# Two small gaps in on-chip memory: the arena moved by 64 bytes and the weight buffers by 96, in a 256-token transformer kernel

## The reference

```
# first block
p = rms_norm(x) @ w_in                 # 2048 -> 5632 and 8 gate columns
y = mixers(p) @ w_out                  # gated delta rule, RG-LRU, SGU, short conv; 2048 -> 2048
x = x + rms_norm(y)
y = (gelu(gate) * val) @ ffn_down      # gate, val = conv(rms_norm(x) @ ffn_up); 2048 -> 2*5632 -> 2048
x = x + rms_norm(y)
# second block
x = x + 0.5 * swiglu(rms_norm(x), ffn1_w_gate, ffn1_w_up, ffn1_w_down)
proj = rms_norm(x) @ w_in_2            # dilated and differential attention, two gates
y = sigmoid(g_dil) * (o_dil @ w_dil_branch) + sigmoid(g_diff) * (o_diff @ w_diff_branch)
x = x + y @ w_out_2
x = x + 0.5 * swiglu(rms_norm(x), ffn2_w_gate, ffn2_w_up, ffn2_w_down)
```

## Time and profile before

| | |
|---|---|
| time, median of three runs | 3381.89 us |
| profiled execution, first to last instruction | 3379.9 us |
| PE busy | 3364.0 us |
| DVE / ACT / POOL busy | 2240.8 / 1745.9 / 533.6 us |
| DMA | 616 MB, mean share of the 16 DMA engines about 57% |
| granted TensorE clock, mean | 0.999 |

### The profile page before, as it was taken

One profiled execution on the slowest core, in us unless ns is written; L12 is line 12 of the kernel. 1 busy time (PEld: TensorE's weight loads), 2 busy tenths in 40 slices (PEclk: granted clock), 3 DMA queues, 4 the chain that ended last, 5 costly groups with the idle time before them and its releaser, 6 DMA issues.

```text
span 3379.9 us, 59341 instructions
## 1 busy us (share of the span) xinstructions
PE 3364.0 (100%) x19746; PEld 2935.0 (87%) x19746; DVE 2240.8 (66%) x2874; ACT 1745.9 (52%) x2588; POOL 533.6 (16%) x502
## 2 busy tenths in 40 slices
PE   9999999999999999999999999999999999999999
PEld 8888888888888888888888888888888888888888
DVE  7878587777744565656555599766687655655544
ACT  5555665555544554454444555554565554444433
POOL 0214111111100011111100066511100111111000
PEclk9999999999999999999999999999999999999999
DMA  6534555555566555555566655545566555555665
GB/s 212 162 113 156 185 170 186 187 190 188 183 193 189 175 179 191 187 189 187 186 190 187 217 176 174 190 154 160 168 195 197 189 187 189 187 186 192 183 193 171
DMA packets 176036, 616.21 MB, mean 182 GB/s; under 512 B 20912, under 2 KB 21584, under 8 KB 175568
## 3 DMA queue, kind: packets, MB, share of 16 engines
q1 hardware_dynamic: 175520, 609.84, 56.6%
q10 hardware_dynamic: 432, 5.24, 0.4%
HBM read 610.81 MB, written 4.19 MB: 182 GB/s over the span
## 4 chain that ended last, share of the span: by engine, by line
PE 94%; DVE 3%; issue 1%; ACT 1%; SPq 1%; DMA 0%; POOL 0%; DVEq 0%; POOLq 0%; ACTq 0%
PE acc L461 60%; PE acc L464 30%; DVE weights_low L311 1%; PE ps_wide L390 1%; PE acc L476 1%; ACT weights_high L304 0%; PE ps_narrow L2550 0%; PE ps_wide L2526 0%; PE acc L479 0%; DVE halves_memory L566 0%; DMA weights_raw<-in_w_in 0%; DMA weights_raw<-in_w_diff_branch 0%; DVE halves_memory L3009 0%; PE ps_scale L2931 0%; PE ps_wide L2537 0%
## 5 line engine op out<-in xcount | busy, mean ns | idle before, releaser
L461 PE MATMUL acc<-moving_halves,weights_high 128*128 128x512 f32 x6304 | 1994.5, 398 | 1.7 <-DVE x_T L2819 1.7
L311 DVE TENSOR_TENSOR weights_low<-weights_raw,weights_high 128x1024 fp32r<-128x1024 f32 (+1 forms) x1172 | 1433.8, 1236 | 728.4 <-ACT weights_high L304 726.8
L304 ACT ACTIVATE weights_high<-weights_raw 128x1024 fp32r<-128x1024 f32 (+1 forms) x1172 | 1208.5, 1032 | 786.0 <-PE acc L464 756.1
L464 PEld LDWEIGHTS acc<-moving_halves,weights_low 128*128 128x128 f32 x6304 | 1184.9, 188 | 280.1
L464 PE MATMUL acc<-moving_halves,weights_low 128*128 128x256 f32 x6304 | 1239.7, 278 | 0.0
L461 PEld LDWEIGHTS acc<-moving_halves,weights_high 128*128 128x128 f32 x6304 | 962.9, 189 | 12.0 <-issue 9.8
L461 PE MATMUL acc<-gated_halves,weights_high 128*128 128x512 f32 x2024 | 635.6, 395 | 0.0
L560 ACT ACTIVATE cross_products<-acc 128x256 f32<-128x256 f32 x503 | 192.5, 383 | 678.6 <-PE acc L464 678.5
L464 PEld LDWEIGHTS acc<-gated_halves,weights_low 128*128 128x128 f32 x2024 | 380.2, 188 | 89.9
L583 POOL TENSOR_TENSOR stage_scratch<-unscaled,token_scale 128x256 f32<-128x256 f32 x260 | 215.6, 829 | 1293.6 <-DVE unscaled L566 811.8
L464 PE MATMUL acc<-gated_halves,weights_low 128*128 128x256 f32 x2024 | 397.6, 278 | 0.0
(11 more groups left out here) (384 smaller groups left out, 2011.1 us busy)
## 6 DMA issues: line engine op xcount, KB each, us to landing
weights_raw<-in_w_in SPq DMA_DIRECT2D x268, 512.0 KB, 3.9
weights_raw<-in_ffn_up SPq DMA_DIRECT2D x176, 512.0 KB, 4.4
weights_raw<-in_ffn_w_gate SPq DMA_DIRECT2D x176, 512.0 KB, 4.1
weights_raw<-in_ffn_w_up SPq DMA_DIRECT2D x176, 512.0 KB, 4.7
weights_raw<-in_ffn_w_down SPq DMA_DIRECT2D x160, 512.0 KB, 3.8
weights_raw<-in_ffn_down SPq DMA_DIRECT2D x80, 512.0 KB, 3.8
weights_raw<-in_w_out SPq DMA_DIRECT2D x64, 512.0 KB, 4.1
weights_raw<-in_ffn_w_down SPq DMA_DIRECT2D x32, 256.0 KB, 2.7
```

The lines of the kernel that those rows point to most:

```text
L304: core.nc.scalar.activation(core.high[:, slot, k0:nk, :].rearrange("p a b -> p (a b)"), core.raw[:, slot, k0 * P:nk * P], ACT.Copy).then_i ...
L311: core.nc.vector.tensor_tensor(core.low[:, slot, k0:nk, :].rearrange("p a b -> p (a b)"), core.raw[:, slot, k0 * P:nk * P], core.high[:, s ...
L461: core.nc.tensor.matmul(acc[:, t % 2, :, :], core.high[:, u % SLOTS, k, :], parts[:, prod.first[t] + k0 + k, :, :], start=(k0 + k == 0), s ...
L464: core.last = core.nc.tensor.matmul(acc[:, t % 2, 0, :], core.low[:, u % SLOTS, k, :], parts[:, prod.first[t] + k0 + k, 0, :], start=False ...
```

## The change

Two unused buffers are allocated: 64 bytes a partition in front of the arena and 32 bytes in front of the weight buffers. All that follows them moves. No instruction is added, removed or reordered on any engine; operand addresses alone differ.

```diff
         self.h = self.over(self.h_at, "moving_halves", KT)
 
+        self.sb("before_arena", [P, 16], F32)
         self.arena_at = nc.sbuf_base
         self.arena = self.sb("arena", [P, ARENA_TILES, S], F32)
         self.g_parts = self.over(self.arena_at, "gated_halves", FF_TILES)
         self.y_parts = self.over(self.arena_at + 28 * S * 4, "gated_branch_halves", KT)
+        self.sb("before_weights", [P, 8], F32)
         self.raw = self.sb("weights_raw", [P, SLOTS, KG * P], F32)
         self.high = self.sb("weights_high", [P, SLOTS, KG, P], F32R)
         self.low = self.sb("weights_low", [P, SLOTS, KG, P], F32R)
```

## The result

The changed kernel takes 3407.08 us (median of 5 runs, 3405.46 to 3410.55), the kernel before 3381.89 us; the ratio is 1.0079, with a 95% interval of 1.0066 to 1.0091. I had forecast 3363 us, with a range up to 3404. The profiled execution went from 3379.9 to 3403.6 us, 23.7 us more.

The account below looks back on a forecast made before the run. PE's own pace, start to start of matmuls, was taken to bound the kernel. Quartets -16.7 and sextets -1.8 gave -18.5 us on 3379.9, 3361.4; with 2.0 us from profiled span to median, 3363 us, range 3312 to 3404.

Parts of the forecast that it names:

- small buffers: Constants, vectors and scratch move by 96 bytes; mostly plain fp32 matmuls read them; taken as nothing.
- splits: Splits of weight chunks on ACT and DVE, 1056 and 1268 ns; even 10% more would be hidden; taken as nothing.
- DMA: Landings of weight chunks in weights_raw; even half slower, by 2.4 us, they would still fit; taken as nothing.
- starts off 64: Weight rows start at 224, 32 past a multiple of 64; taken as no change in weight loads, upper end left open.
- the nearest row: Quartets on mixed_halves at distance 320, taken as guide for 4388 quartets going to 96 or 32: 3.8 ns each, -16.7 us.
- Sextets: 44 on gated_halves gain 40 ns each, -1.8 us; 8 on mixed_halves may lose 40 ns each, 0.3 us.
- The slower one: Rival for quartets on moving_halves and gated_halves: moving stream runs into weights; +45 us, 3427, or a quarter, 3404; chance 0.23.
- The larger gain: Rival: a distance suiting the quartet brings half the bound, 13.5 ns on 4388 quartets, -59 us, 3323 us; chance 0.22.
- the 27 ns: Best bound for a quartet: the sextets' 6.7 ns on each of four matmuls, -118 us over 4388 quartets.
- a quarter of a bound: Upper end of the range, 3404 us: the quarter of the slower case, +22 us over 4508 quartets.

Follow-up runs that it names:

- the one that left it where it was: Against the kernel before, weights_high and weights_low moved by 192 bytes and weights_raw stayed in place: 3357.28 us, ratio 0.9927.
- the runs by 96: Two kernels against the one before: all buffers moved by 96 bytes, 3380.92 us, ratio 1.000; the weight buffers alone by 96, 3413.23 us, ratio 1.0092.

## Why the prediction was wrong

**What bounds the kernel, and what can change.** Right. It is PE's pace, and no wait, no other engine and no transfer. That small buffers, splits, DMA and starts off 64 cost nothing is shown by the run with all buffers moved by 96 (ratio 1.000), and for the place of weights_raw once more by the one that left it where it was.

**"I read this as the moving stream and the weight load [...] by an amount that depends on where the two start relative to each other".** Right in that the distance matters: the runs by 96 separate it from the starts themselves. That the two reads get in each other's way in SBUF remains my reading; the runs show what the pace depends on, not where in the chip the time goes. By the Trainium skill ("TensorE: Matmul & The Clock Gate", "Step-by-step: what each phase is for") loading weights takes no read bandwidth from the running matmul. As I read it, no shift should have moved the time; shifts moved it from 3356 to 3413 us.

**"The value I take is the nearest row, a quartet whose rows start apart: 693.1 ns for 696.9."** This is the step that failed. It took distance 320 for any distance that isn't 0. The measured curve is not "together or apart" but goes up and down with a period of 256 bytes, and 320 is 64 on it, one of the two good odd multiples, while the change goes to 96 and 32, two of the three bad ones of the eight places. Measured +6.6 ns (moving_halves) and +6.0 ns (the others) in place of -3.8: 3152 x 6.6 + 1236 x 6.0 = 28.2 us in place of -16.7. "A start that coincides is the special one" was an argument without a row; 0 is a middling place.

**Sextets.** The sign was right on gated_halves (720 to 710 ns, a gain of 0.4 us for 1.8), and mixed_halves lost 31 ns each, as allowed for. I was misled in using them as "the clearer comparison". A quartet isn't made of four sextet matmuls: at distance 64 the sextet is at its best (680 ns), the quartet isn't (693.5 against 690.4 at 192); at 128 the sextet gains 8 ns (712) and the quartet nothing.

**Starts off a multiple of 64.** Right: the run by 96 shows it (1.000). The Trainium skill ("SBUF — State Buffer", "Specifications (TRN2)") has lines of 16 bytes and a penalty for each crossing into a new one. I had taken from it that a shift by whole lines changes nothing. For the starts alone the run by 96 agrees; for the distance that reading fails, since 16 bytes cost 9.6 ns a quartet.

**The rivals.** The slower one gave 3427 us in full and 3404 at a quarter; measured 3407, so the quarter was about its size; I gave it 0.23. Its picture, in which the moving stream runs into weights a little ahead of it, isn't borne out: by it 64, between 32 and 96, would lose as well, and 64 gains (693.5 ns). The larger gain (half of the 27 ns) exists, at 192, but is 6.3 ns.

**Absorption.** I let every quartet count. 28.2 + 1.1 (mixed_halves) less 0.4 (sextets) is 29 us; 23.7 arrived, the rest being taken up in the two stages with other work between the quartets.

**The range** reached 3404. Two measured places of a curve, both favourable to change, carried a range whose upper part was a quarter of a bound. With one good point known and nothing of the rest, the honest likeliest case was that bad places are as frequent as good ones.

## What to carry to other kernels

In this kernel, where PE streams fp32r matmuls back to back with a weight load for each, the start of the weight rows less that of the moving rows, mod 256, is a parameter worth 16.7 ns in 700 (2.4% between the best and the worst of eight places), and it shows in no busy share: read start-to-start intervals of a repeated pattern. In another kernel of this kind, sweep it with a pad in front of the weight buffers, which costs only the bytes, in steps of 32 first and of 16 around the best; here 192 gave 3356.4 us. Look at each stage and at several runs, since a stage can fall into a second pace at the same addresses. Don't infer one place of such a curve from another, and don't take a different mix of matmul sizes as its proxy.

## What the runs showed of the hardware

- The mean pace of an fp32r quartet depends on the distance mod 256 bytes, from 690.0 to 706.7 ns, and not on the absolute starts in the one pair that tests it (696.7 with all starts at 128 and with all at 224).
- At one distance whole stages can still differ: 703.3 and 706.7 ns at 96 within one launch, sextets of 680 and 707 ns at 192.
- 16 bytes matter: 690.4 ns at 192, 700.0 at 208.
- A 256-column fp32r matmul with its own weight load is never faster than some 113 ns from start to start in any run; at the distances 0 to 224 in steps of 32 (sextets on gated_halves) it was 120, 118, 113, 119, 119, 120, 116 (the mean of 113 and 118) and 117.
- Plain fp32 matmuls of line 390 show no such effect: 379 ns at the median for both kinds of starts, and 216 ns from start to start in the kernel before, in the changed one, with all buffers moved by 96 and with the weights moved by 192.
- Counted at one column a cycle of the full 2.4 GHz clock, a quartet's 1536 columns would be 640 ns. Even at the best distance it takes 50 ns more. What the rest is, and whether 640 can be reached, no run here tells.
